# Differential and latent attention, its units issued three deep: a new order of issue on four engines, and another spread of the second gate's additions

## The reference, cut to what matters

```python
s1 = einsum('bhqd,bhkd->bhqk', q1, k1) * DA_SCALE      # differential: halves of 64
s2 = einsum('bhqd,bhkd->bhqk', q2, k2) * DA_SCALE
w = softmax(s1) - lam * softmax(s2)
o_da = einsum('bhqk,bhkd->bhqd', w, v)
...
s = einsum('bhqd,bhkd->bhqk', q, k) * scale             # latent: 128 + 64 rope
o_mla = einsum('bhqk,bhkd->bhqd', softmax(s), v)
...
mod_x = silu(c) @ w_ada + b_ada                          # six parts of 2048; the last is the gate g2
x = x + g2 * conv_ffn(h2, ...)
```

## Time and profile before

| what | value |
|---|---|
| median of 3 runs | 3177.64 us (3173.39 to 3178.29) |
| the profiled execution | 3180.76 us |
| its span | 3178.9 us |
| TensorE busy | 2911.0 us, 92% |
| VectorE busy | 1804.0 us, 57% |
| ScalarE busy | 1191.1 us, 37% |
| GpSimd busy | 165.0 us, 5% |
| attention stage | from about 500 to 660 us |

### The profile page before, as it was taken

The page is one execution under the profiler, slowest core; times in us unless marked ns, Lnnn a source line. Parts: engine busy times, 40 slices in busy tenths (PEclk is TensorE's granted clock), DMA queues, the critical chain, the costliest instruction groups (busy, mean ns, idle before and its releaser), DMA issues.

```text
span 3178.9 us, 35028 instructions
## 1 busy us (share of the span) xinstructions
PE 2911.0 (92%) x13848; PEld 2378.0 (75%) x13848; DVE 1804.0 (57%) x2015; ACT 1191.1 (37%) x1134; POOL 165.0 (5%) x338
## 2 busy tenths in 40 slices
PE   5888895778999999999799999998879899999997
PEld 2587673467888888888587888887768788888886
DVE  1385776664555645555455557984754544555553
ACT  2232213433444434344344434333333343444332
POOL 0000005200000000000000100015300000000000
PEclk8999897999999999999889999999989999999999
DMA  8687875535456565546354876665236456555554
GB/s 333 245 293 259 304 255 185 179 132 192 164 172 206 174 210 186 184 162 206 96 199 169 269 224 215 223 201 167 60 120 207 150 164 207 199 189 193 169 174 134
DMA packets 347323, 617.34 MB, mean 194 GB/s; under 512 B 51232, under 2 KB 102064, under 8 KB 339776
## 3 DMA queue, kind: packets, MB, share of 16 engines
q1 hardware_dynamic: 310320, 582.69, 55.2%
q10 hardware_dynamic: 36880, 32.94, 3.1%
HBM read 586.57 MB, written 29.00 MB: 194 GB/s over the span
## 4 chain that ended last, share of the span: by engine, by line
PE 79%; DVE 11%; DMA 4%; ACT 3%; issue 2%; SPq 0%; POOL 0%; ACTq 0%; DVEq 0%; POOLq 0%
PE ps L306 21%; PE ps L307 21%; PE ps L308 21%; DVE w_lo L269 3%; PE ps L974 2%; PE ps L975 2%; PE ps L976 2%; DMA raw<-in_pack_ada 1%; DVE upd L2155 1%; PE ps L1199 1%; PE ps L587 1%; DVE w_lo L754 1%; DMA proj_q<-stg 1%; PE ps L2453 1%; PE ps L385 1%
## 5 line engine op out<-in xcount | busy, mean ns | idle before, releaser
L269 DVE TENSOR_TENSOR w_lo<-raw,w_hi 128x2048 fp32r<-128x2048 f32 (+3 forms) x428 | 892.0, 2094 | 703.7 <-ACT w_hi L262 702.4
L262 ACT ACTIVATE w_hi<-raw 128x2048 fp32r<-128x2048 f32 (+3 forms) x428 | 745.1, 1753 | 785.1 <-PE ps L308 728.0
L306 PE MATMUL ps<-w_hi,a_hi 128*128 128x512 f32 (+1 forms) x2272 | 892.2, 393 | 17.2 <-DVE a_lo L626 7.0
L308 PE MATMUL ps<-w_hi,a_lo 128*128 128x512 f32 (+1 forms) x2272 | 885.9, 390 | 0.0
L307 PE MATMUL ps<-w_lo,a_hi 128*128 128x512 f32 (+1 forms) x2272 | 885.6, 390 | 0.0
L306 PEld LDWEIGHTS ps<-w_hi,a_hi 128*128 128x128 f32 x2272 | 431.1, 190 | 109.8 <-DVE a_lo L626 8.7
L308 PEld LDWEIGHTS ps<-w_hi,a_lo 128*128 128x128 f32 x2272 | 430.8, 190 | 88.8
L307 PEld LDWEIGHTS ps<-w_lo,a_hi 128*128 128x128 f32 x2272 | 431.0, 190 | 85.6
L306 PE MATMUL ps<-w_hi,b_hi 128*128 128x512 f32 x864 | 339.0, 392 | 10.6 <-DVE w_lo L269 5.7
L308 PE MATMUL ps<-w_hi,b_lo 128*128 128x512 f32 x864 | 337.5, 391 | 0.0
L307 PE MATMUL ps<-w_lo,b_hi 128*128 128x512 f32 x864 | 337.4, 391 | 0.0
(11 more groups left out here) (319 smaller groups left out, 2788.3 us busy)
## 6 DMA issues: line engine op xcount, KB each, us to landing
raw<-in_hyb_w_in SPq DMA_DIRECT2D x96, 1024.0 KB, 5.3
raw<-in_sc_w_in SPq DMA_DIRECT2D x96, 1024.0 KB, 5.1
raw<-in_w_up SPq DMA_DIRECT2D x88, 1024.0 KB, 5.0
raw<-in_pack_ada SPq DMA_DIRECT2D x96, 512.0 KB, 6.2
raw<-in_w_down SPq DMA_DIRECT2D x48, 768.0 KB, 4.4
raw<-in_w_in SPq DMA_DIRECT2D x24, 1024.0 KB, 7.3
raw<-in_hyb_w_out SPq DMA_DIRECT2D x32, 768.0 KB, 4.5
raw<-in_sc_w_out SPq DMA_DIRECT2D x32, 768.0 KB, 4.4
```

Of the source, the lines that this page charges most:

```text
L262: nc.scalar.activation(w_hi[s][:, 0:n_k, 0:ncols], raw[s][:, 0:n_k, 0:ncols], ACT.Copy).then_inc(sem("hi_done"), 1)
L269: nc.vector.tensor_tensor(w_lo[s][:, 0:n_k, 0:ncols], raw[s][:, 0:n_k, 0:ncols], w_hi[s][:, 0:n_k, 0:ncols].bitcast(F32), ALU.subtract).th ...
L306: nc.tensor.matmul(o, h, w_hi[s][:, k, 0:ncols], start=kt == 0, stop=False)
L308: last = nc.tensor.matmul(o, l, w_hi[s][:, k, 0:ncols], start=False, stop=kt == L.groups[-1][0] + L.groups[-1][1] - 1)
```

## The change

TensorE, ScalarE and VectorE now go through the stage by a step v from 0 to 33. In step v, TensorE issues the scores of unit v, the transposes of unit v - 2, in odd steps the flip of the next head, and the product with v of unit v - 2. ScalarE issues the copy of the transposed weights of v - 2, in odd steps the copies of q and k and the loads of the head two further on, and the exponentials of v. VectorE issues the maximum of v, the weights of v - 1, the output of v - 2 and then as many additions for the second gate as `G2_ADDS` says: one and two in turn in the differential half, three a unit in the latent half up to unit 28, one in unit 29 and none after. `att_weights` has one more wait, for the output of unit u - 2, which reads the same column of `mx`. SyncE loads the row blocks by the count of additions done, still after the v load of a head. The hardware loops of TensorE and ScalarE give way to straight code. GpSimd keeps its loops.

```diff
--- before.py
+++ after.py
@@ -1095,10 +1095,14 @@
             for kt in range(4):
                 g2_load(sp, kt)
             gate_bias_load(sp, 1)
+            loaded = RING
             for h in range(2, 2 * HEADS):
                 att_load_v(sp, h)
-                if h + 2 < KT:
-                    g2_load(sp, h + 2)
+                while loaded < KT and loaded < g2_rows(2 * h - 2) + RING:
+                    g2_load(sp, loaded)
+                    loaded += 1
+            for kt in range(loaded, KT):
+                g2_load(sp, kt)
             for g, (kt, n_k) in enumerate(WO.groups):
                 sp.wait_ge(sem("late_used"), N_UNITS + KT - RING + g + 1)
                 load_piece(sp, WO, WO.p0 + g, kt, n_k, 0)
@@ -1200,16 +1204,12 @@
                                         stop=k == n_keys - 1)
             last.then_inc(sem("at_pv"), 1)
 
-        def att_head_pe(pe, h, i=None, flip_next=True):
-            att_scores(pe, h, 0, i)
-            if h >= 1:
-                att_wt(pe, 2 * h - 1, i)
-                att_pv(pe, 2 * h - 1, i)
-            att_scores(pe, h, 1, i)
-            if flip_next:
-                att_flip(pe, h + 1, i)
-            att_wt(pe, 2 * h, i)
-            att_pv(pe, 2 * h, i)
+        LAST_U = 4 * HEADS
+
+        def flips_in(v):
+
+            h = (v + 1) // 2
+            return h if v % 2 and h < 2 * HEADS else None
 
         def over_heads(eng, emit, chain=None, per=0):
 
@@ -1231,9 +1231,15 @@
             last.then_inc(sem("kr_flip"), 1)
             pe.wait_ge(sem("at_dve"), 2)
             att_flip(pe, 0)
-            over_heads(pe, lambda h, i=None: att_head_pe(pe, h, i, h != 2 * HEADS - 1))
-            att_wt(pe, 4 * HEADS - 1)
-            att_pv(pe, 4 * HEADS - 1)
+            for v in range(LAST_U + 2):
+                if v < LAST_U:
+                    att_scores(pe, v // 2, v % 2)
+                if v >= 2:
+                    att_wt(pe, v - 2)
+                if flips_in(v):
+                    att_flip(pe, flips_in(v))
+                if v >= 2:
+                    att_pv(pe, v - 2)
             g2_total(pe)
 
         def att_qT(act, h, i=None):
@@ -1272,33 +1278,23 @@
             nc.scalar.activation(wT[u % 2][:].rearrange("p k q -> p (k q)"), ps[:, 6, :], ACT.Copy
                                  ).then_inc(sem("at_wT"), 1)
 
-        def att_head_act(act, h, i=None):
-            if h >= 1:
-                att_wT(act, 2 * h - 1, i)
-            att_exp(act, 2 * h, i)
-            if h != 2 * HEADS - 1:
-                att_qT(act, h + 1, i)
-                att_kT(act, h + 1, i)
-            att_wT(act, 2 * h, i)
-            att_exp(act, 2 * h + 1, i)
-            if h < 2 * HEADS - 3:
-                att_load_qk(act, h + 3, i)
-
         def att_act(act):
             act.wait_ge(sem("at_dve"), 1)
             nc.scalar.activation(lamt[:, 0:2], lamt[:, 2:4], ACT.Exp).then_inc(sem("act_once"), 1)
             att_qT(act, 0)
             att_kT(act, 0)
             att_load_qk(act, 2)
-
-            att_head_act(act, 0)
-            for first, straight in ((1, (5, 6, 7, 8)), (HEADS + 1, (13, 14, 15))):
-                with act.Fori(0, 2) as i:
-                    att_head_act(act, first, i)
-                    att_head_act(act, first + 1, i)
-                for h in straight:
-                    att_head_act(act, h)
-            att_wT(act, 4 * HEADS - 1)
+            for v in range(LAST_U + 2):
+                if v >= 2:
+                    att_wT(act, v - 2)
+                h = flips_in(v)
+                if h:
+                    att_qT(act, h)
+                    att_kT(act, h)
+                    if h + 2 < 2 * HEADS:
+                        att_load_qk(act, h + 2)
+                if v < LAST_U:
+                    att_exp(act, v)
             act.wait_ge(sem("at_dve"), 3)
             nc.scalar.activation(ssum[:], ssum[:], ACT.Sqrt, bias=C["eps"], scale=1.0 / HD).then_inc(sem("act_once"), 1)
 
@@ -1315,6 +1311,8 @@
             latent = u >= 2 * HEADS
             par = u % 2
             dve.wait_ge(sem("at_exp"), ev2(u + 1, i))
+            if u >= 2:
+                dve.wait_ge(sem("at_o"), u - 1)
             n = 1 if latent else 2
             if latent:
 
@@ -1333,19 +1331,17 @@
             dst = o_all[:, t, bass.ds(head_col(h, i, HD), HD)]
             nc.vector.tensor_scalar(dst, ps[:, 7, 0:HD], mx[t][:, 6:7], None, ALU.mult).then_inc(sem("at_o"), 1)
 
-        def att_head_dve(dve, chain, h):
-
-            att_max(dve, chain, 2 * h)
-            if h >= 1:
-                att_out(dve, 2 * h - 1)
-            g2_add(dve, h, 0)
-            att_weights(dve, chain, 2 * h)
-            att_max(dve, chain, 2 * h + 1)
-            g2_add(dve, h, 1)
-            att_weights(dve, chain, 2 * h + 1)
-            g2_add(dve, h, 2)
-            att_out(dve, 2 * h)
-            g2_add(dve, h, 3)
+        G2_ADDS = [1, 2] * HEADS + [3] * 13 + [1, 0, 0]
+        assert sum(G2_ADDS) == ADA_COLS * KT
+
+        def g2_rows(u):
+
+            return sum(G2_ADDS[:u + 1]) // ADA_COLS
+
+        def g2_adds(dve, u):
+            first = sum(G2_ADDS[:u])
+            for n in range(first, first + G2_ADDS[u]):
+                g2_add(dve, n // ADA_COLS, n % ADA_COLS)
 
         def att_dve(dve, chain):
             dve.wait_ge(sem("at_tab"), 16 * 7)
@@ -1360,9 +1356,15 @@
 
             chain.done(nc.vector.tensor_tensor(lamt[:, 2:3], lamt[:, 1:2], lamt[:, 0:1], ALU.subtract))
             chain.done(nc.vector.tensor_scalar(C["lam"], lamt[:, 2:3], -LAMBDA_INIT, None, ALU.add))
-            for h in range(2 * HEADS):
-                att_head_dve(dve, chain, h)
-            att_out(dve, 4 * HEADS - 1)
+            for v in range(LAST_U + 2):
+                if v < LAST_U:
+                    att_max(dve, chain, v)
+                if 1 <= v <= LAST_U:
+                    att_weights(dve, chain, v - 1)
+                if v >= 2:
+                    att_out(dve, v - 2)
+                if v < LAST_U:
+                    g2_adds(dve, v)
 
             dve.wait_ge(sem("at_o"), 4 * HEADS)
             da = o_all[:, :, 0:DA_W]
```

## The result

The changed kernel takes 3156.5 us, the median of 5 runs (3151.27 to 3160.42), against 3177.64 before. The ratio is 0.993, with a 95% interval of 0.9919 to 0.9942. The forecast was 3155.5. The profiled execution took 3157.95 us with a span of 3156.0 us.

The account below looks back on a forecast made before the run. VectorE's work was taken to bound the differential half, TensorE's chain the latent half. Gains of 14.7 + 7.6 = 22.3 us took the profiled 3180.76 to 3158.5, 3155.5 as a median; range 3148 to 3168.

Parts of the forecast that it names:

- VectorE's waits in the differential half: VectorE, differential heads: 4.7 us idle before the reciprocal and 1.4 before the output, per 53 us, should go.
- 8.3 us a head: Differential heads, paced by VectorE: 8.3 us each in place of 10.33, giving 16.2 us over eight heads.
- the start: Filling the pipe at the first differential units: 1.5 us taken off the gain, leaving 14.7.
- TensorE's turn of 7.3 us: TensorE's work per differential head: 7.3 us at full clock, 1.0 less than VectorE's, so it keeps up.
- The additions: VectorE's second-gate additions, 0.817 us each in differential heads: they fall from four to three a head.
- The latent half: Scores of unit 16 to the end, paced by TensorE at 8.2 us a head: 70.1 against 77.7, gaining 7.6 us.
- the odd unit's 4.21: TensorE's time for an odd latent unit: scores, transposes, flip covering the weights' copy, product; 4.21 us.
- the rival with a new wait of TensorE's: TensorE's order brings its own wait, 0.9 us a unit in one half, losing 14 of 22 us: 3169, chance 0.08.
- The clock: TensorE's granted clock: reckoned full, 1.00 after the first 15 us; a fall in every head (3163) had chance 0.14.
- the busy share of 80%: TensorE busy 6.6 of 8.3 us per differential head, given as the reason to reckon with full clock.
- Loads: Loads of q, k, v and gate rows: all hidden, the tightest gate row having 9 us against a 5.1 us landing.
- the rival with late rows: SyncE's gate rows 10 to 15 land late, the stage growing by 6L - 37 at L us each: 3190, chance 0.04.

Follow-up runs that it names:

- the second profile: The changed kernel run once more with nothing changed, for the spread of what lies outside attention: 3158.22 us, ratio 0.9932 to the kernel before.

## Why the prediction was right, point by point

*VectorE's waits in the differential half.* Right. Over the whole half the waits before the reciprocal and the output were 8.7 and 3.3 us, and 0 and 0.5 are left: 11.5 us. With 5.7 for the eight additions, and 1.3 and 0.3 for one unit's weights and one output that now come after the maximum of unit 16, that is 18.8 us, against 18.4 measured. The run with the weights first brings 5.1 us of the first wait back. The prediction put the whole of it down to VectorE's order, one unit of time for the exponentials; by that run and the old order with three additions most of it had already gone with the rest of the new order, 14.4 to 5.1.

*8.3 us a head.* Right for the steady part, by the profile: after the first four units the maxima of the changed kernel go from 514.14 (unit 4) to 563.96 (unit 16), 49.8 us for six heads. The term that was mis-sized is the start. I took 1.5 us off for filling the pipe; instead the first two heads took 14.3 us, less than two times 8.3, because in this order the first step has no weights and the first two no output, and those come after the maximum of unit 16. In the second profile they took 16.1, so there was some cost of filling in that one. So the half was put at 67.9 us and measured 64.2 by that mark. Part of these 3.7 us is work that only crossed the mark I had chosen.

*TensorE's turn of 7.3 us.* Right: it doesn't show in the changed kernel, and with half an addition a unit, where TensorE is the bound, a head takes 7.1.

*The additions.* Right. Moving one out of the differential half is worth 0.72 us, or 0.66 to 0.81 by the steady units (forecast 0.817, the duration of one). That this needs the new order wasn't said in the prediction; in the old order eight of them bring 0.4 us.

*The latent half.* The place was right, but the gain is 2.4 us less than forecast: 72.5 us where the sum gave 70.1. The failing term is the odd unit's 4.21. The sum set the copy of k, 1.16 us, equal to the product, 1.16, and the profile shows 0.29 us of waiting and 0.24 us more in the first scores, less 0.19 by which the product is shorter on the chain: 8.53 us a head for 8.2, seven times. This was named as the weak point in the rival with a new wait of TensorE's, and it came at 0.3 us a head, not at 0.9 a unit. The run with the flip one unit earlier gets all of it back and more, down to 68.8, since the hole goes and the shorter product stays.

*What gained in the latent half* was the flip's place and not the third unit: two units in flight with the flip behind the transposes reach 72.4. The prediction's sum said as much without saying it, since each of its terms was TensorE's own order. What it didn't see is that the new order, three units deep, is what lets the flip stand there in the differential half too; with two units that costs 9.6 us.

*The clock.* Right. The granted clock was 0.99 over the differential half for 0.85 before, and 1.00 in every window after the start. By the rule of the Trainium skill that spoke against it (TensorE: Matmul & The Clock Gate, section HAM oscillation) a fall in each head was to be feared; after the start no fall came in either profile of the changed kernel. The prediction's reason, the busy share of 80%, isn't shown to be what held the clock: it also held after the stretch with 2.92 of 5 us, while before it fell after one with 2.62. The second profile of the changed kernel has a mean of 0.94 and a differential half 1.4 us longer; both differences lie at the start, and whether the one explains the other wasn't tried. Nor is the clock what made the old half long: the kernel before, its straight code and the version with the flip behind in latent heads have a mean granted clock of 0.85, 0.91 and 0.81 over a differential half of 82.6, 82.6 and 82.7 us.

*Loops.* Right to give them nothing: 1.1 us of the stage, not to be seen in the total.

*Loads.* Right. The landing of a gate row rose from 5.1 to 7.0 us in the median. The tightest one, row 10, took 7.5 of its 9 us; the next, issued right behind it, took 10.1, and no addition waited for it. (In the rival with late rows, the prediction's own formula gives 6.7 us slower at L = 11, not 6.4.)

*The total.* 14.7 + 7.6 = 22.3 against 18.4 + 5.2 less 1.0 for the two marks, 22.6. Two errors of opposite sign, 3.7 and 2.4, make the total look better than its terms. That the median came within 1.0 us of the forecast is luck on top of that: the rest of the program alone differs by up to 12 us from one profile to another.

## What to carry to other kernels

Before deepening a pipeline, ask of each wait whether it is one of distance (another engine needs time, and a further unit of other work between them covers it) or one of order (an engine does A before B though only B is waited for); the second is mended by moving one block, here for a quarter of the whole gain with no third unit. The two are not independent: a block that may stand anywhere in a deep pipeline can close a circle in a shallow one. And filler work that covers a wait is worth moving only once that wait is gone: eight additions were worth 0.4 us before and 5.7 us after.

## What the runs showed of the hardware that wasn't expected

Some of VectorE's instructions that work on SBUF alone take longer while GpSimd works on its rope. Two of the combined weights in the timeline of the changed kernel:

```profile
528.97 1.20 DVE L1325 SCALAR_TENSOR_TENSOR wt<-ex,mx 128x512 f32<-128x512 f32 x1
...
553.99 0.75 DVE L1325 SCALAR_TENSOR_TENSOR wt<-ex,mx 128x512 f32<-128x512 f32 x1
```

GpSimd is busy from 528.89 to 530.76 us and idle from 550.48 to 556.27. All four weights of this kernel that fall wholly into GpSimd's idle time take 0.75 us; the ten that fall almost wholly into its busy time take 0.75 to 1.20, 0.94 in the mean. The additions show the same, 836 ns in the stretch 520 to 560 us and 748 in the latent half, where GpSimd has less to do: 0.09 us an addition in the mean. The operation after the maximum takes 0.17 us with GpSimd idle and up to 0.67 beside it. The reciprocals (0.16 us), the other small operation (0.27) and the maxima, which read PSUM (1.21), do not change. The Trainium skill (SBUF — State Buffer, section Who interferes with whom) says that a VectorE instruction with two inputs in SBUF contends with a GpSimd instruction that reads SBUF, and for the weights and the additions the trace agrees. What the half would be without this wasn't tried.
